# Two of four float32 value units of an attention projection on TensorE's float16 path

## The chip, the core and the metric

The kernel runs on one core of one Trainium2 chip. The metric is the device time of one execution in microseconds (us); lower is better.

## The reference, cut to what matters

One step of a two-layer decoder trunk, for a prompt of 256 tokens and 8 samples of one new token each (past length 256), with shared weights, all in float32. Layer 0 uses sparse softmax attention (8 heads of 128; a ReLU indexer picks 64 keys for each query and the rows are gathered, for the samples from a paged cache), layer 1 an RG-LRU. A ConvGLU follows each, with RMSNorms before and one at the end. The part around the change is this:

```python
q, k, v, qi, ki, wi = jnp.split(a @ w_in, ATTN_SPLITS, axis=-1)   # a: (256 + 8 tokens, 1024)
q, k = rope(q, pos), rope(k, pos)                                 # also qi, ki
idx, valid = indexer_topk(qi, wi, ki, q_pos, n_keys, 64)
logits = einsum(q, gather(k, idx)) * HEAD_DIM ** -0.5             # invalid: -inf
o = einsum(softmax(logits), gather(v, idx))
```

## The kernel before

The 264 tokens lie in the free dimension, the features in the partitions. Every projection is cut into **units** of 128 output columns: one unit is one PSUM bank of `acc` (128x264), summed over 8 chunks of 128 input features. The 27 units of the attention's input projection are ordered by hand in `ORDER`: 0 to 8 are the indexer and q0 to q5, 9 and 10 are v0 and v1, 11 and 12 are q6 and q7, 13 to 16 are v2 to v5, 17 to 24 are k0 to k7, and 25 and 26 are v6 and v7. Units 27 to 34 are the output projection.

**A normal unit** multiplies in float16 halves. SyncE loads the float32 weights (512 KB) into one of four slots of `stage`. ScalarE makes the high half, float16(512 w), in `hi` (L593). VectorE makes the low half, float16(512 w - high), in `lo` (L997). TensorE then runs three float16 matmuls for each chunk, 24 in all: high by `aH`, high by `aL`, low by `aH` (`unit`, L1535, L1538, L1541).

**A raw unit** (`RAW_V`, units 13 to 16) skips both halves: its weights go straight to `raw_v`, and TensorE multiplies them in float32 with `x32`, a float32 copy of the normalized input that ScalarE makes a chunk at a time (L786). That is 8 matmuls of two records each in the trace (`unit_raw`, L1506). All four are loaded together once a scratch area is free, and share the semaphore `raw_in` (L462).

**Each engine walks a loop over steps u**, one for each unit, and does in that step what the hand-made order gives it; each engine executes strictly in order. What matters around the change:
- TensorE: unit u, then the small matmuls and transposes of the step. `heads_of_step(u)` turns one value or key head token-major (L1616, L1617): v0 at step 11, v1 at 12, v2 at 14, v3 at 15, v4 at 16, k0 to k7 at steps 19 to 26. Before the n-th such turn it waits until ScalarE has copied out the one before (`kv_kept`). For a value it waits too until ScalarE has evicted its unit (`v_read`). `turn_picked` (L1706) spreads the samples' picked row numbers inside unit 14. `spread_queries` runs inside unit 15, `turn_weights` inside unit 22, `sample_values` inside units 23 and 24.
- ScalarE: `swap_halves(u)` (L703, L704) for the rotary embedding of a q or k unit, `keep_turned` (L691) for the turn of the step before, `keep_v(u)` (L714, L715) for a value unit, then `hi(u+4)`. Step 12 starts with three parameter copies (L772, L774), step 13 with `qrep` (L778), which waits until q7 is rotated.
- VectorE: `rope(u)` (L1080, L1081) multiplies with cosine and sine; `take_merged` (L1105 to L1109) does eight rounds of max, index and replace that find the samples' 64 keys, the eighth in step 11 after `rope(12)`; `take_second` does the same for the prompt; `sample_dots(j)` (L1136), steps 15, 16, 16 and 17, multiplies gathered keys with the samples' queries; then `lo(u+4)`.
- GpSimd: the subtraction that ends a rotation (L2046, signals `roped`), in step 12 also `row_numbers` (L2026 to L2030, signals `phys_done`), which needs the last round of `take_merged`; in step 16 the eight gathers of cache rows (L2020), the four of values after unit 16 is done.

The four matmul banks are reused in turn, so unit u also waits until bank u - 4 has been read.

Of the kernel before, what the change touches and what calls it, by code (L numbers as in the profile page):

```python
# [16 lines left out]
ALU = mybir.AluOpType  # L17
ACT = mybir.ActivationFunctionType
# [7 lines left out]
D = 1024  # L26
# [38 lines left out]

RAW_V = U_V[2:6]
SPLIT_AT = {u: u - SLOTS for u in range(SLOTS, U_OUT + SLOTS) if u not in RAW_V}

# [114 lines left out]
def build(nc, a, o):  # L183
    with ExitStack() as ctx:
# [92 lines left out]
        kxT = area1[:, 4608:4608 + D].rearrange("p (r n) -> p r n", r=8)  # L277

        spareH = zH[:, DC:FC, :].rearrange("p c t -> p (c t)").bitcast(F32)
        spareL = zL[:, DC:FC, :].rearrange("p c t -> p (c t)").bitcast(F32)  # L280
# [112 lines left out]
        idx_mm, idx_relu, bias_done = sem("idx_mm"), sem("idx_relu"), sem("bias_done")  # L393
        gidx_done, kx_turned, kx_kept = sem("gidx_done"), sem("kx_turned"), sem("kx_kept")
        kx_in = sem("kx_in")
        kg_in = [sem(f"kg_in{i}") for i in range(4)]
        vg_in = [sem(f"vg_in{i}") for i in range(4)]
        qz_zero = sem("qz_zero")
        ss_mm, ss_relu, sc_mm = sem("ss_mm"), sem("ss_relu"), sem("sc_mm")
# [180 lines left out]
        def _(act):  # L580
# [136 lines left out]
            def after_heads(u):  # L717
# [8 lines left out]
                if LG + 5 <= u and u != INSIDE + 1:  # L726
                    o_high(u - LG - 5)

            for u in range(LAST_STEP + 1):
                if u == 3:  # L730
                    act.wait_ge(unit_done, U_W + 1)
                    nc.scalar.copy(wiT[:], acc[ID:ID + IH, U_W % 4, 0:T]).then_inc(wi_kept, 1)
# [12 lines left out]
                if u == 6:  # L745
                    act.wait_ge(qz_zero, 1)
                    act.wait_ge(roped, 3)
                    for half in range(2):
                        rows_ = slice(ID * half, ID * half + ID)
                        places = qz[rows_, :].rearrange("p (s m) -> p m s", s=NS)  # L750
                        for b in range(2):
                            ins = nc.scalar.copy(places[:, b:b + 3:2, :], qiT[ID * b:ID * b + ID, :, TP:T])
                    ins.then_inc(ki_twice, 1)
                    act.wait_ge(idx_mm, 2)
                    nc.scalar.activation(relu0[:, 1::2, :], E[:, TP:2 * TP].rearrange("p (h k) -> p h k", h=2), ACT.Relu).then_inc(idx_relu, 1)
# [45 lines left out]
                if u < U_OUT and u not in U_V:  # L801
                    swap_halves(u)
                if u == 21:
                    act.wait_ge(smx_done, 1)
                    nc.scalar.activation(sl[:], sl[:], ACT.Exp).then_inc(sexp_done, 1)
# [182 lines left out]
        def _(dve):  # L988
# [157 lines left out]
            for u in range(LAST_STEP + 1):  # L1146
# [4 lines left out]
                if u == 3:  # L1151
                    dve.wait_ge(roped, 3)
                    v.tensor_copy(kiT[ID:P, :], kiT[0:ID, :]).then_inc(ki_twice, 1)
                if u == 22:
                    dve.wait_ge(sp_turned, 1)
# [84 lines left out]
                if u == 11:  # L1240
                    take_merged(6, 1)
                    rope(12)
                    take_merged(7, 1, found=True)
                if 16 <= u < 18:
                    sample_dots(u - 14)
                if u == 20:

# [240 lines left out]
        def _(pe):  # L1488
# [10 lines left out]
            def unit_raw(u, between):  # L1499
# [9 lines left out]
                ins.then_inc(unit_done, 1)  # L1509

            def unit(u, xH, xL, bank=None, first=True, last=True, x0=0, ready=None, rest_ready=None, between=None):

                n, cols = shape(u)
                if u in RAW_V:
                    unit_raw(u, between)
                    return
# [234 lines left out]
            for u in range(2, U_OUT + 1):  # L1751
                if u == 3:
                    pe.wait_ge(x_kept, 2)
                if u < U_OUT:
                    if u in (23, 24):
                        between = lambda i: sample_values(4 * (u - 23) + i // 4, i % 4)
                    elif u == 5:
                        between = lambda i: index_products() if i == 6 else None
                    elif u == 6:
                        between = lambda i: late_scores() if i == 4 else None  # L1760
                    elif u == 14:
                        between = lambda i: turn_picked() if i == 8 else None
                    elif u == 15:
                        between = lambda i: spread_queries() if i == 4 else None
                    elif u == 22:
                        between = lambda i: turn_weights() if i == 8 else None
# [41 lines left out]
                if u != INSIDE:  # L1808
                    heads_of_step(u)
                if u == 20:  # L1810
                    pe.wait_ge(qb_read, 4)
# [107 lines left out]
        def _(pool):  # L1919
# [34 lines left out]
            g.memset(ones[:], 1.0).then_inc(ones_set, 1)  # L1954
            g.memset(qz[:], 0.0).then_inc(qz_zero, 1)
            pool.wait_ge(pages_in, 32)
            g.tensor_scalar(gidx[:], ptc[:], 8.0, blkc[:, 0:1], ALU.mult, ALU.add).then_inc(gidx_done, 1)
            pool.wait_ge(gidx_done, 1)
            g.indirect_dma_start(out=kx, out_offset=None, in_=a["cache_kidx"].rearrange("a n (b r) d -> (a n b) (r d)", b=8),
# [72 lines left out]
            def biases():  # L2032
# [7 lines left out]
                g.tensor_scalar(seld[:], ident[0:NS, 0:NS], selnew[:, 0:1], None, ALU.mult).then_inc(phys_done, 1)  # L2040

            for u in range(LG + 1 + H):
                if u < U_OUT and u not in U_V:
                    dst, part = roped_home(*KIND[u])
# [127 lines left out]
```

## Time and profile before

| | |
|---|---|
| median of 3 runs | 591.82 us (591.76 to 592.20) |
| the profiled execution | 592.18 us |
| its span, first to last instruction | 590.4 us |
| instructions | 12747 |
| TensorE busy / VectorE / ScalarE / GpSimd | 579.4 / 453.6 / 369.7 / 226.8 us |
| mean granted TensorE clock | 0.996 of full speed |
| HBM read, written | 108.8 MB, 3.9 MB |

A matmul's busy time overlaps the next one's, since matmuls are pipelined; the pitch from one start to the next tells what it costs. Times in a timeline count from the start of the span. The stretch of the change is 44 to 110 us, units 9 to 25.

### The profile page before, as it was taken

How to read it: one execution, taken by the hardware profiler on the slowest of the kernel's cores; microseconds unless marked ns; L12 is line 12 of the kernel's file. 1: busy time of each engine (PE TensorE's matmuls, PEld its weight loads, DVE VectorE, ACT ScalarE, POOL GpSimd, SP SyncE). 2: the span in 40 equal slices, each digit the busy share in tenths (PEclk: the TensorE clock that was granted, in tenths of full speed). 3: DMA queues.
4: the chain of work that ended last, by engine and by line, in shares of the span. 5: the costliest groups of instructions: out<-in, count | busy, mean ns of one | idle time of the engine just before them, and what ended most of it. 6: DMA issues, size and time to landing. Idle time of an engine off the chain costs nothing.

```text
span 590.4 us, 12747 instructions
## 1 busy us (share of the span) xinstructions
PE 579.4 (98%) x5015; PEld 502.8 (85%) x5015; DVE 453.6 (77%) x904; ACT 369.7 (63%) x629; POOL 226.8 (38%) x230
## 2 busy tenths in 40 slices
PE   7999999999999999999999999999999999999995
PEld 7888889888888888888888888888888888888885
DVE  4899996666897778787778898789878777885542
ACT  6985566676765666575555788856756566654322
POOL 4241466713354544551000112273644555432220
PEclk9999999999999999999999999999999999999998
DMA  9959694329766766678997952065766666879602
GB/s 264 263 137 278 184 339 133 108 80 324 209 200 194 198 195 195 197 226 244 259 264 216 239 170 73 1 179 172 207 193 199 192 195 199 233 220 240 175 7 74
DMA packets 205420, 113.28 MB, mean 192 GB/s; under 512 B 5561, under 2 KB 202217, under 8 KB 205337
## 3 DMA queue, kind: packets, MB, share of 16 engines
q1 hardware_dynamic: 203169, 106.33, 63.9%
q0 software_dynamic: 1680, 5.79, 2.8%
q8 instruction: 40, 0.66, 0.5%
q10 hardware_dynamic: 512, 0.35, 0.2%
q14 instruction: 19, 0.16, 0.1%
HBM read 108.83 MB, written 3.86 MB: 191 GB/s over the span
## 4 chain that ended last, share of the span: by engine, by line
PE 92%; DVE 3%; POOL 1%; ACT 1%; issue 1%; DVEq 0%; ACTq 0%; POOLq 0%
PE acc L1538 25%; PE acc L1535 25%; PE acc L1541 25%; PE acc L1506 2%; PE acc L1726 1%; PE acc L1728 1%; PE acc L1727 1%; PE misc L1897 1%; PE acc L1561 1%; DVE w_lo L997 1%; PE misc L1663 1%; POOL hT L1930 1%; ACT w_hi L593 1%; PE misc L1642 1%; PE misc L1626 1%
## 5 line engine op out<-in xcount | busy, mean ns | idle before, releaser
L1535 PE MATMUL acc<-aH,w_hi 128*128 128x264 f16 (+1 forms) x886 | 244.5, 276 | 0.8 <-DVE work L1310 0.7
L1538 PE MATMUL acc<-aL,w_hi 128*128 128x264 f16 (+1 forms) x886 | 244.5, 276 | 0.0
L1541 PE MATMUL acc<-aH,w_lo 128*128 128x264 f16 (+1 forms) x886 | 244.5, 276 | 0.0
L997 DVE SCALAR_TENSOR_TENSOR w_lo<-stage,w_hi 128x1024 f16<-128x1024 f32 (+1 forms) x155 | 205.7, 1332 | 30.4 <-ACT w_hi L593 29.9
L593 ACT ACTIVATE w_hi<-stage 128x1024 f16<-128x1024 f32 (+1 forms) x155 | 171.1, 1109 | 32.4 <-PE acc L1541 25.2
L1535 PE MATMUL acc<-zH,w_hi 128*128 128x264 f16 x384 | 106.0, 276 | 0.0
L1538 PE MATMUL acc<-zL,w_hi 128*128 128x264 f16 x384 | 106.0, 276 | 0.0
L1541 PE MATMUL acc<-zH,w_lo 128*128 128x264 f16 x384 | 106.0, 276 | 0.0
L1538 PEld LDWEIGHTS acc<-aL,w_hi 128*128 128x128 f16 (+1 forms) x886 | 88.1, 99 | 13.5
L1535 PEld LDWEIGHTS acc<-aH,w_hi 128*128 128x128 f16 (+1 forms) x886 | 86.8, 98 | 14.5 <-issue 1.5
L1541 PEld LDWEIGHTS acc<-aH,w_lo 128*128 128x128 f16 (+1 forms) x886 | 88.1, 99 | 12.6
L2016 POOL TENSOR_TENSOR scratch<-work,r0z 128x264 f32<-128x264 f32 x44 | 65.5, 1488 | 75.2 <-ACT work L891 75.2
L2014 POOL COPY ftail<-scratch 128x10 f32<-128x10 f32 x44 | 49.1, 1116 | 35.3 <-DVE scratch L1328 35.0
L885 ACT ACTIVATE work<-scratch,fprm 128x264 f32<-128x264 f32 x44 | 26.7, 608 | 48.8 <-DVE scratch L1328 48.6
L1328 DVE TENSOR_TENSOR scratch<-acc,rinv 128x264 f32<-128x264 f32 x44 | 19.0, 432 | 39.3 <-PE acc L1541 39.2
L1535 PEld LDWEIGHTS acc<-zH,w_hi 128*128 128x128 f16 x384 | 37.6, 98 | 5.6
L1541 PEld LDWEIGHTS acc<-zH,w_lo 128*128 128x128 f16 x384 | 37.6, 98 | 5.6
L1538 PEld LDWEIGHTS acc<-zL,w_hi 128*128 128x128 f16 x384 | 37.6, 98 | 5.6
L891 ACT ACTIVATE work<-work 128x264 f32<-128x264 f32 x44 | 18.6, 423 | 35.0 <-DVE work L1341 35.0
L1946 POOL TENSOR_TENSOR sqsum<-sqsum,sq 128x264 f32<-128x264 f32 x18 | 16.0, 886 | 54.6 <-ACT sq L615 54.0
L607 ACT ACTIVATE aH<-hT,gcol 128x264 f16<-128x264 f32 x24 | 12.3, 514 | 32.7 <-DVE hT L1361 18.2
L2046 POOL TENSOR_TENSOR area<-area,scratch 128x264 f32<-128x264 f32 x16 | 17.6, 1102 | 31.4 <-DVE area L1081 31.4
(421 smaller groups left out, 951.7 us busy)
## 6 DMA issues: line engine op xcount, KB each, us to landing
stage<-in_w_ffn_up SPq DMA_DIRECT2D x88, 512.0 KB, 4.7
stage<-in_w_ffn_down SPq DMA_DIRECT2D x32, 704.0 KB, 5.7
stage<-in_w_attn_in SPq DMA_DIRECT2D x22, 512.0 KB, 6.6
stage<-in_w_rec_in SPq DMA_DIRECT2D x16, 512.0 KB, 4.9
stage<-in_w_attn_out SPq DMA_DIRECT2D x8, 512.0 KB, 3.8
stage<-in_w_rec_out SPq DMA_DIRECT2D x8, 512.0 KB, 3.8
area<-in_w_attn_in SPq DMA_DIRECT2D x4, 512.0 KB, 4.6
area<-in_x_prompt SPq DMA_DIRECT2D x2, 512.0 KB, 4.6
```

The lines of the kernel that those rows point to most:

```text
L593: nc.scalar.activation(halves_of(u)[0], stage[:, s, 0:n, 0:cols], ACT.Copy, scale=WSCALE).then_inc(hi_done, 1)
L885: nc.scalar.activation(c32[:, p, :], gs[:, p, :], ACT.Identity, scale=fprm[layer][:, FROW_W + 2, j:j + 1], bias=fprm[layer][:, FROW_B, j:j ...
L891: nc.scalar.activation(c32[:, p, :], c32[:, p, :], ACT.Gelu_apprx_tanh).then_inc(gelu_done, 1)
L997: v.scalar_tensor_tensor(low, stage[:, place_in_line(u) % 4, 0:n, 0:cols], WSCALE, high, ALU.mult, ALU.subtract).then_inc(lo_done, 1)
L1328: v.tensor_tensor(gs[:, p, :], acc[:, u % 4, 0:T], rinv[:], ALU.mult).then_inc(acc_read, 1)
L1535: t_.matmul(out, high[:, c, :], xH[:, x0 + c, :], start=first and c == 0, stop=False)
L1538: t_.matmul(out, high[:, c, :], xL[:, x0 + c, :], start=False, stop=False)
L1541: ins = t_.matmul(out, low[:, c, :], xH[:, x0 + c, :], start=False, stop=last and c == n - 1)
L1946: g.tensor_tensor(sqsum[:], sqsum[:], sq[:, c % 2, :], ALU.add).then_inc(ss_done, 1)
L2014: g.tensor_copy(ftail[:, :, j], gs[:, p, TP - 2:T]).then_inc(tail_copied, 1)
L2016: g.tensor_tensor(gr[:, p, :], c32[:, p, :], r0z[:], ALU.mult).then_inc(gr_done, 1)
L2046: g.tensor_tensor(dst, dst, rot[0:part, (before(u) + 1) % 2, :], ALU.subtract).then_inc(roped, 1)
```

## The change

Units 13 and 14 (v2, v3) stop being raw. Their weights are still loaded raw, with the two that stay raw, in `raw_v`. ScalarE makes both high halves in step 11. GpSimd makes the low half of v2 in two passes (multiply by 512 in place, then subtract) and half of the low half of v3. VectorE makes the other half of v3's in one instruction, after `rope(12)`. The halves lie in a part of `zH` and `zL` that is idle then. TensorE multiplies them in float16, all 16 high products first and the 8 low ones after. `turn_picked`, two of the four `sample_dots`, the samples' softmax, `turn_weights` and `sample_values` move up to a unit later. Two semaphores are renamed or replaced to make room.

```diff
+HALVED_V = RAW_V[:2]
...
+        half_v = [[z[:, 0:DC, :].rearrange("p c t -> p (c t)")[:, j * D:(j + 1) * D].rearrange("p (c n) -> p c n", c=DC)
+                   for z in (zH, zL)] for j in range(len(HALVED_V))]
...
+            def high_of_value(j):
+
+                act.wait_ge(raw_in, 16 * len(RAW_V))
+                nc.scalar.activation(half_v[j][0], raw_v[:, j], ACT.Copy, scale=WSCALE).then_inc(v_hi, 1)
+
             for u in range(LAST_STEP + 1):
+                if u == 11:
+                    high_of_value(0)
...
                 if u == 6:
-                    act.wait_ge(qz_zero, 1)
+                    act.wait_ge(mask_set, 1)
...
                 if u < U_OUT and u not in U_V:
                     swap_halves(u)
-                if u == 21:
+                if u == 11:
+                    high_of_value(1)
+                if u == 22:
                     act.wait_ge(smx_done, 1)
                     nc.scalar.activation(sl[:], sl[:], ACT.Exp).then_inc(sexp_done, 1)
...
-                if u == 22:
+                if u == 23:
                     dve.wait_ge(sp_turned, 1)
...
                 if u == 11:
                     take_merged(6, 1)
                     rope(12)
+                    dve.wait_ge(v_hi, 2)
+                    dve.wait_ge(v_lo, 1)
+                    v.scalar_tensor_tensor(half_v[1][1][:, DC // 2:, :], raw_v[:, 1, DC // 2:, :], WSCALE, half_v[1][0][:, DC // 2:, :],
+                                           ALU.mult, ALU.subtract).then_inc(v_lo, 1)
                     take_merged(7, 1, found=True)
-                if 16 <= u < 18:
-                    sample_dots(u - 14)
-                if u == 20:
+                if u in (17, 19):
+                    sample_dots(2 + (u - 17) // 2)
+                if u == 21:
...
+            def unit_value(u, j):
+
+                high, low = half_v[j]
+                out = acc[:, u % 4, 0:T]
+                pe.wait_ge(v_hi, j + 1)
+                bank_free(u)
+                for c in range(DC):
+                    t_.matmul(out, high[:, c, :], aH[:, c, :], start=c == 0, stop=False)
+                    t_.matmul(out, high[:, c, :], aL[:, c, :], start=False, stop=False)
+                pe.wait_ge(v_lo, 1 + 2 * j)
+                for c in range(DC):
+                    ins = t_.matmul(out, low[:, c, :], aH[:, c, :], start=False, stop=c == DC - 1)
+                ins.then_inc(unit_done, 1)
...
-                    if u in (23, 24):
-                        between = lambda i: sample_values(4 * (u - 23) + i // 4, i % 4)
+                    if u in (24, 25):
+                        between = lambda i: sample_values(4 * (u - 24) + i // 4, i % 4)
...
-                    elif u == 14:
-                        between = lambda i: turn_picked() if i == 8 else None
                     elif u == 15:
-                        between = lambda i: spread_queries() if i == 4 else None
-                    elif u == 22:
+                        between = lambda i: turn_picked() if i == 2 else spread_queries() if i == 4 else None
+                    elif u == 23:
                         between = lambda i: turn_weights() if i == 8 else None
...
-                if u == 20:
+                if u == 21:
                     pe.wait_ge(qb_read, 4)
...
-            g.memset(qz[:], 0.0).then_inc(qz_zero, 1)
+            small(g.memset(qz[:], 0.0))
...
+            def low_of_value(j, chunks):
+
+                pool.wait_ge(v_hi, j + 1)
+                small(g.tensor_scalar(raw_v[:, j, chunks, :], raw_v[:, j, chunks, :], WSCALE, None, ALU.mult))
+                g.tensor_tensor(half_v[j][1][:, chunks, :], raw_v[:, j, chunks, :], half_v[j][0][:, chunks, :],
+                                ALU.subtract).then_inc(v_lo, 1)
+
             for u in range(LG + 1 + H):
+                if u == 11:
+                    low_of_value(0, slice(0, DC))
+                if u == 12:
+                    low_of_value(1, slice(0, DC // 2))
                 if u < U_OUT and u not in U_V:
                     dst, part = roped_home(*KIND[u])
                     pool.wait_ge(acc_read, before(u) + 1)
```

## Rows read from the trace of the kernel before

**Rows 1.** The page: busy time, share of the span and instructions.
```profile
PE 579.4 (98%) x5015; PEld 502.8 (85%) x5015; DVE 453.6 (77%) x904; ACT 369.7 (63%) x629; POOL 226.8 (38%) x230
```

**Rows 2.** Waits of PE from 50 to 130 us (total us, times, longest).
```profile
PE misc L1616 <- DVE zL L1128: 0.4, 1, 0.4
```

**Rows 3.** PE's timeline, units 12 to 15 (start us, duration).
```profile
54.26 0.27 PE L1535 MATMUL acc<-aH,w_hi 128*128 128x264 f16 x1
...
56.96 0.27 PE L1616 MATMUL misc<-ca,scratch 128*128 128x128 f32 x1
...
57.17 3.06 PE L1506 MATMUL acc<-scratch,area 128*128 128x264 f32 x13
...
60.74 2.39 PE L1506 MATMUL acc<-scratch,area 128*128 128x264 f32 x10
...
64.91 0.27 PE L1616 MATMUL misc<-ca,scratch 128*128 128x128 f32 x1
```

**Rows 4.** Line L462 (raw loads), window 47.7 to 48.9 us.
```profile
L462 SPq DMA_DIRECT2D area<-in_w_attn_in x2: 380/771/1162, 47.4 to 47.8; - x2
...
DMA to landing us min/median/max: 4.4/4.9/5.5
```

**Rows 5.** ACT's timeline, steps 11 to 13.
```profile
50.85 0.52 ACT L786 ACTIVATE r0z<-hT,gcol_w 128x264 f32<-128x264 f32 x1
53.20 0.38 ACT L703 COPY scratch<-acc 64x264 f32<-64x264 f32 x1 [1.84 <-PE acc L1541]
...
53.98 0.95 ACT L772 COPY fprm<-misc 128x440 f32<-128x440 f32 x2
...
55.14 0.40 ACT L691 COPY area<-misc 128x256 f32<-128x256 f32 x1
...
60.03 1.14 ACT L778 COPY area<-area 128x512 f32<-128x512 f32 x2 [2.12 <-POOL area L2046]
...
61.41 0.39 ACT L715 ACTIVATE scratch<-acc 128x264 f32<-128x264 f32 x1
61.68 1.06 ACT L593 ACTIVATE w_hi<-stage 128x1024 f16<-128x1024 f32 x1
```

**Rows 6.** POOL's timeline, steps 8 to 18.
```profile
46.30 0.74 POOL L2046 TENSOR_TENSOR area<-area,scratch 128x264 f32<-128x264 f32 x1 [1.15 <-DVE area L1081]
57.19 0.74 POOL L2046 TENSOR_TENSOR area<-area,scratch 128x264 f32<-128x264 f32 x1 [10.15 <-DVE area L1081]
59.26 0.74 POOL L2046 TENSOR_TENSOR area<-area,scratch 128x264 f32<-128x264 f32 x1 [1.33 <-DVE area L1081]
...
62.08 0.44 POOL L2030 TENSOR_SCALAR zL<-idxf 8x64 f32<-8x64 f32 x1
...
83.26 1.66 POOL L2046 TENSOR_TENSOR area<-area,scratch 128x264 f32<-128x264 f32 x1 [2.67 <-DVE area L1081]
```

**Rows 7.** Groups of POOL instructions, shapes apart (busy us, mean ns).
```profile
L1999 POOL TENSOR_TENSOR fpre<-fprm 128x176 f32<-128x176 f32 x2 | 1.1, 560 | 0.0
...
L1981 POOL TENSOR_SCALAR eps<-eps 128x264 f32<-128x264 f32 x1 | 0.9, 881 | 0.1
...
L1972 POOL TENSOR_SCALAR pt8f<-pt 8x2 f32<-8x2 int32 x1 | 0.2, 228 | 0.0
```

**Rows 8.** Line L2071 of POOL, window 122.0 to 122.5 us (ns min/median/max).
```profile
L2071 POOL TENSOR_SCALAR work<-work,prcp,r0tok x2: 447/500/553, 122.1 to 122.5; 128x128 f32<-128x128 f32 x1, 128x256 f32<-128x256 f32 x1
```

**Rows 9.** DVE's timeline, steps 8 and 11.
```profile
46.34 1.78 DVE L997 SCALAR_TENSOR_TENSOR w_lo<-stage,w_hi 128x1024 f16<-128x1024 f32 x1
...
56.34 0.43 DVE L1080 TENSOR_TENSOR scratch<-scratch,ca 128x264 f32<-128x264 f32 x1
...
58.41 0.43 DVE L1080 TENSOR_TENSOR scratch<-scratch,ca 128x264 f32<-128x264 f32 x1
```

**Rows 10.** PE's timeline, the turn of k1 in step 20.
```profile
85.66 0.27 PE L1616 MATMUL misc<-ca,area 128*128 128x128 f32 x1
```

More of the change, by code:

```diff
@@ L393, in build @@
         idx_mm, idx_relu, bias_done = sem("idx_mm"), sem("idx_relu"), sem("bias_done")
-        gidx_done, kx_turned, kx_kept = sem("gidx_done"), sem("kx_turned"), sem("kx_kept")
+        v_hi, kx_turned, kx_kept = sem("v_hi"), sem("kx_turned"), sem("kx_kept")
         kx_in = sem("kx_in")
@@ L397, in build @@
         vg_in = [sem(f"vg_in{i}") for i in range(4)]
-        qz_zero = sem("qz_zero")
+        v_lo = sem("v_lo")
         ss_mm, ss_relu, sc_mm = sem("ss_mm"), sem("ss_relu"), sem("sc_mm")
@@ L1509, in unit_raw @@
                 ins.then_inc(unit_done, 1)
+            def unit_value(u, j):
[10 more added lines that the diff above has]
+                ins.then_inc(unit_done, 1)
             def unit(u, xH, xL, bank=None, first=True, last=True, x0=0, ready=None, rest_ready=None, between=None):
                 n, cols = shape(u)
+                if u in HALVED_V:
+                    unit_value(u, HALVED_V.index(u))
+                    return
                 if u in RAW_V:
@@ L1954, in _ @@
             g.memset(ones[:], 1.0).then_inc(ones_set, 1)
-            g.memset(qz[:], 0.0).then_inc(qz_zero, 1)
+            small(g.memset(qz[:], 0.0))
             pool.wait_ge(pages_in, 32)
-            g.tensor_scalar(gidx[:], ptc[:], 8.0, blkc[:, 0:1], ALU.mult, ALU.add).then_inc(gidx_done, 1)
-            pool.wait_ge(gidx_done, 1)
+            small(g.tensor_scalar(gidx[:], ptc[:], 8.0, blkc[:, 0:1], ALU.mult, ALU.add))
             g.indirect_dma_start(out=kx, out_offset=None, in_=a["cache_kidx"].rearrange("a n (b r) d -> (a n b) (r d)", b=8),
```

## The prediction

> **What bounds the kernel now.** Look first at the busy shares on the page: TensorE is busy for 579.4 us of the 590.4 us span [rows 1]. Then ask for TensorE's waits in the stretch of the change: from 50 to 130 us it waits once, for 0.4 us [rows 2]. So every microsecond taken from TensorE's own work is a gain there, and every new wait of TensorE is a loss of its full length. The work around it can only do harm. The third view is therefore each engine's timeline from unit 11 to unit 15, where I follow the change.
>
> **What TensorE saves.** Unit 12 shows the float16 price: 54.26 to 56.96, 2.70 us for 24 matmuls [rows 3]. Raw unit 13 runs from 57.17 to the start of unit 14 at 60.74, 3.57 us. Two units change form: 2 x (3.57 - 2.70) = **1.74 us saved**. Unit 14 with `turn_picked` takes until 64.91, so that spread costs 4.17 - 3.57 = 0.60 us; it moves to unit 15 at the same price. The turns and later sample products keep their prices too, a unit later.
>
> **ScalarE, first new wait.** Both high halves wait for all four raw loads. The last is issued at 47.8 and lands 5.5 us later, at 53.3 [rows 4]. ScalarE is ready at 50.85, where its last x32 chunk stood; that chunk now queues behind the first high half [rows 5]. In order: high half of v2, 1.06 us (the row of L593), to 54.36; the x32 chunk 0.52, to 54.88; the swap of q6, 0.78 (53.20 to 53.98), to 55.66; high half of v3, 1.06, to 56.72; the parameter copies 1.16 (53.98 to 55.14), to 57.88; and the copy of turned v0, 0.40, to 58.28 instead of 55.54. TensorE wants to turn v1 at 56.96 and needs that copy gone: it waits **1.32 us**, where it had 1.4 us to spare. (Neighbouring copies overlap by up to 0.1 us, so 1.1 is as likely.) Unit 13 then starts at 57.17 + 1.32 = 58.49.
>
> **GpSimd, what a pass costs.** No row shows 128x1024 elements on this engine. For the two-input pass: 176 columns take 0.56 us [rows 7] and 264 take 0.74 [rows 6], 2.05 ns a column and 0.20 fixed, so 1024 columns take 2.3 us and 512 take 1.25. Its second input is float16, which no row has; I take it as float32. For the one-input multiply by a constant, the same form is L1981: 264 columns in 0.88 us, against 0.23 for two columns, so 2.5 ns a column [rows 7]; 1024 columns are 2.78 us, 512 are 1.5. The other end is L2071, whose factors are per-partition operands: 0.45 us for 128 columns, 0.55 for 256 [rows 8], 0.83 ns a column, so 1.2 us and 0.77. I take L1981, since its operands have the form of the new instruction, and keep L2071 for the other end.
>
> The Trainium skill ("GPSIMD Engine Reference", § 4.1 Engine selection) calls one-input work roughly line-rate, which speaks for the cheap end; L1981 disagrees and L2071 agrees. By the page the sum would be the 0.9 us of the second case below.
>
> **GpSimd against VectorE.** At 46.34 VectorE's low half takes 1.78 us: a GpSimd subtraction had begun at 46.30 and ran to 47.04, and VectorE finished 1.08 us after that [rows 6, 9]. So one of these blocks the other for its whole length. The new passes and `rope(11)`, `rope(12)` and VectorE's half of v3 will take turns. By this I place the work:
> - GpSimd multiplies v2 from 54.37 to 57.15. `rope(11)`, due at 56.34 [rows 9], goes first after that, to 57.58. GpSimd subtracts from 57.58 to 59.9: `v_lo` is 1.
> - VectorE needs 2.07 us from one rope to the next (56.34 to 58.41), so it is ready for `rope(12)` at 59.2, waits to 59.9, ends its first product at 60.35. GpSimd's subtraction of q6 runs to 61.1. VectorE's half of v3 (half of 1.08, some 0.6) runs to 61.7.
> - GpSimd multiplies half of v3, 61.7 to 63.2, and subtracts, 63.3 to 64.55: `v_lo` is 3. The subtraction of q7 ends at 65.3. Before, it ended at 60.0 [rows 6]; it is 5.3 us late.
>
> Without turn-taking it would end at about 63.9, so blocking is 1.4 us of this. The Trainium skill ("SBUF — State Buffer", § Who interferes with whom) states the same exclusive lock for a VectorE instruction with two SBUF inputs against a GpSimd one that reads SBUF; the 1.78 us row agrees.
>
> **What TensorE then waits for.** Unit 13 needs `v_lo` 1 after its 16 high products, at 58.49 + 1.80 = 60.3: it has been there since 59.9, no wait. Unit 14 starts at 61.19 and needs `v_lo` 3 at 62.99: it comes at 64.55, **1.56 us**. It ends at 65.45. Next is the turn of v2, which needs ScalarE's `keep_v` of unit 13. ScalarE stands at `qrep`, which waits for q7's subtraction, with the copy of v1 and `keep_v` queued behind it. Before, from 60.00 to the end of L715 at 61.80 that is 1.80 us [rows 5, 6]. Now 65.3 + 1.8 = 67.1, so **1.65 us** more. Unit 15 starts at 67.32 (a turn is 0.21: 56.96 to 57.17). Before it would have started, without the 0.60 of `turn_picked`, at 65.12 - 0.60 = 64.52.
>
> **Sum.** 1.32 + 1.56 + 1.65 - 1.74 = **2.8 us lost** at unit 15.
>
> **Behind unit 15.** `row_numbers` ends 2.5 us after q7's subtraction (60.00 to 62.52), so at 67.8; `turn_picked` comes at 67.32 + 2 x 0.45 = 68.2. No wait, where the old place would have waited. Picks and cache gathers are then some 5.2 us later than before (`turn_picked` stood at 60.74 + 5 x 0.45 = 63.0), TensorE only 2.8. The tightest follower is the turn of k1 at 85.66, whose subtraction on GpSimd ended at 84.92 [rows 6, 10]: 0.74 us of slack. The moved `sample_dots` leave before `rope(17)` and `rope(18)` one set of dots less each, some 1.9 us (8 x 0.21 and the bias), so I cost this part at nothing. What hides it is that slack and that move, and if both are gone the last rival's price is due. VectorE's added 0.6 us goes the same way. The samples' softmax, exponent and weights shift together with their readers by one unit: nothing. The changed start-up semaphores: GpSimd idles for 10.15 us before 57.19 and far more at the start, nothing.
>
> **The numbers.** The profiled execution has a span of 590.4 us and a time of 592.18, 1.78 outside the span, and is 0.36 above the median of the runs. The span becomes 593.2, that execution 595.0, the median 591.82 + 2.8 = **594.6 us**. A measurement of this kernel can tell about 0.2% from no change, 1.2 us.
>
> **The cases.**
> 1. *As summed*, 594.6 (593.6 to 595.6): chance 0.53. For it: ScalarE is shown waiting 2.12 us for that subtraction already [rows 5], so any lateness goes through in full.
> 2. *GpSimd multiplies cheaply*, at 1.2 and 0.77 us. The same placing gives: v2's low half at 58.0, `rope(11)` held until then, v3's half at 62.1, VectorE's at 62.7, q7's subtraction at 63.45, the turn of v2 at 65.25, unit 15 at 65.47. That is 0.9 us lost, 592.7: chance 0.22, nearly all of it within 0.2%. It also holds the mix of costlier passes and an earlier landing. If only the ScalarE wait remained, the change would end at 1.32 - 1.74, 0.4 us gained.
> 3. *The conversions hide*, the faster side: copy of v0 by 56.96 and `keep_v` of unit 13 by 57.17 + 5.40 = 62.57. Then no TensorE wait is left and all of the 1.74 us shows: 590.1. It decides at a landing of 52.0 instead of 53.3 and q7's subtraction by 60.8 instead of 65.3. GpSimd's 10.15 us of idle time speaks for it; the placing, in which even the cheap multiply misses by 2.7 us, against it. Chance 0.13.
> 4. *The picks come too late*: the gathers' further 5.2 - 2.8 = 2.4 us go through VectorE's dots to the rotation of k1, less 0.74 of slack: 1.7 us more, 596.3. Chance 0.12.
>
> The range reaches from 591.4 (case 3 out) to 596.0 (most of case 4 in). Faster 0.13; same 0.20, case 2 less its upper edge; slower 0.67.
>
> **What would show it.** In the changed profile: L1506 with 32 records instead of 64, and 48 float16 ones at 0.1125 us pitch. TensorE's list of waits, one row now, should have three new ones: on ScalarE's L691 (about 1.3), on GpSimd's low half in unit 14 (1.6), on ScalarE's L715 (1.7). GpSimd's 128x1024 multiply should take 2.8 us and its subtraction 2.3; `qrep` should start near 65.3. If the multiply is 1.2 us, case 2 holds. If TensorE shows no waits at L1616, the prediction is wrong in sign. If waits sit beyond 80 us, case 4 holds.

## The result and the profile after

| | before | after |
|---|---|---|
| median | 591.98 us (4 runs, 591.76 to 592.20) | 598.99 us (4 runs, 596.66 to 600.32) |
| ratio | | 1.0112 (95%: 1.0100 to 1.0123) |
| profiled execution | 592.18, span 590.4 | 596.66, span 594.9 |

The change costs 7.0 us. The direction was forecast, the size was not: 2.8 us were forecast, and 599.0 lies above the range. The profiled execution of after is the shortest of its four, 2.3 us under the median, so the profile shows only 4.5 of the 7.0 us. The rest is looked for in another profile below.

The page, busy time per engine, to set beside [rows 1]:

```profile
PE 577.8 (97%) x5031; PEld 500.0 (84%) x5031; DVE 457.0 (77%) x905; ACT 371.8 (63%) x631; POOL 234.1 (39%) x234
```

TensorE does 1.6 us less work, as meant. What it waits for in after from 50 to 130 us (total us, times, longest), one row of 0.4 us before [rows 2]:

```profile
PE misc L1649 <- ACT area L694: 3.4, 3, 1.7
PE misc L1649 <- ACT scratch L718: 1.4, 1, 1.4
PE acc L1538 <- POOL zL L2076: 0.4, 1, 0.4
PE misc L1658 <- DVE nmx L1131: 0.3, 1, 0.3
```

PE's timeline says where (start, duration; the bracket is the wait ahead of it). L1649 is the turn, L1616 before [rows 3, 10]:

```profile
58.07 0.30 PE L1649 MATMUL misc<-ca,scratch 128*128 128x128 f32 x1 [1.28 <-ACT area L694]
...
63.38 1.07 PE L1538 MATMUL acc<-aH,zL 128*128 128x264 f16 x8 [0.40 <-POOL zL L2076]
...
65.88 0.33 PE L1649 MATMUL misc<-ca,scratch 128*128 128x128 f32 x1 [1.42 <-ACT scratch L718]
...
89.19 0.30 PE L1649 MATMUL misc<-ca,area 128*128 128x128 f32 x1 [1.72 <-ACT area L694]
...
101.47 0.30 PE L1649 MATMUL misc<-ca,area 128*128 128x128 f32 x1 [0.42 <-ACT area L694]
```

The first three waits are the three forecast ones: the turn of v1, `v_lo` 3 in unit 14, the turn of v2. The last two, at the turns of k1 and k4, lie where the forecast had put nothing. (The 0.3 us on `nmx` comes later still, at 125.7 us.) The same turns give the bill. At the turn of k0 after is 1.64 us behind before (84.39 against 82.75), at k1 3.53 (89.19 against 85.66), at k6 4.48 (114.01 against 109.53), and 4.5 is the difference of the spans.

GpSimd's timeline, the passes that no row of before had shown (compare [rows 6, 7]):

```profile
54.30 2.79 POOL L2075 TENSOR_SCALAR area<-area 128x1024 f32<-128x1024 f32 x1 [7.58 <-ACT zH L735]
57.17 2.13 POOL L2076 TENSOR_TENSOR zL<-area,zH 128x1024 f16<-128x1024 f32 x1
59.25 0.94 POOL L2087 TENSOR_TENSOR area<-area,scratch 128x264 f32<-128x264 f32 x1
60.16 1.93 POOL L2075 TENSOR_SCALAR area<-area 128x512 f32<-128x512 f32 x1
62.17 1.16 POOL L2076 TENSOR_TENSOR zL<-area,zH 128x512 f16<-128x512 f32 x1
63.28 0.74 POOL L2087 TENSOR_TENSOR area<-area,scratch 128x264 f32<-128x264 f32 x1
```

And the late part, in the chain that ended last and on ScalarE's timeline: a load of the stage buffer takes 10.8 us to land, ScalarE's high half waits for it with the copy that TensorE's turn of k1 needs (L694) queued behind. The five input-projection loads that before has from 68 to 92 us take 7.2 us at the median; after's six take 9.3. In before ScalarE waits for no load of the stage from 56 to 100 us.

```profile
76.92 10.78 DMA stage<-in_w_attn_in
```
```profile
87.72 1.06 ACT L596 ACTIVATE w_hi<-stage 128x1024 f16<-128x1024 f32 x1 [2.38 <-DMA stage<-in_w_attn_in]
88.69 0.35 ACT L694 COPY area<-misc 128x256 f32<-128x256 f32 x1
```

Three questions follow. Are the waits in front of unit 15 the change's price, as forecast? What costs 3 us behind it? And why do the runs spread over 3.7 us, when those of before spread over 0.4?

### The profile page after: what moved, and what is told of

Its sections match the earlier page's. It is cut to its first block, busy times and chain, and to the rows that moved or that the text cites. A ratio compares the mean times of both kernels' runs of the same rounds, so it can differ in the third digit from the quotient of the medians.

```text
span 594.9 us, 12788 instructions
## 1 busy us (share of the span) xinstructions
PE 577.8 (97%) x5031; PEld 500.0 (84%) x5031; DVE 457.0 (77%) x905; ACT 371.8 (63%) x631; POOL 234.1 (39%) x234
## 4 chain that ended last, share of the span: by engine, by line
PE 76%; DVE 7%; ACT 6%; DMA 4%; POOL 2%; issue 2%; SPq 1%; ACTq 0%; DVEq 0%
PE acc L1574 23%; PE acc L1571 23%; PE acc L1568 23%; DVE w_lo L1009 3%; ACT w_hi L596 3%; DMA stage<-in_w_attn_in 2%; PE misc L1928 1%; PE acc L1759 1%; PE acc L1761 1%; PE acc L1760 1%; DMA area<-in_w_attn_in 1%; DMA area<-in_x_prompt 1%; POOL area L2075 1%; PE misc L1696 1%; POOL hT L1961 1%
```

## The experiments

Each ratio is against runs of the kernel before on the same chip, whose medians were 591.97 to 592.12. Where the runs of a kernel spread, the ratio differs from the quotient of the two medians. All medians and intervals:

| run | what | us | ratio (95%) |
|---|---|---|---|
| e1_moves | before, the moves alone | 595.68 | 1.0075 (1.0050 to 1.0099) |
| e2_free | after, no conversions | 593.55 | 1.0031 (1.0020 to 1.0042) |
| e3_actfirst | after, ScalarE's copy of qrep last | 596.75 | 1.0082 (1.0065 to 1.0099) |
| e4_again | after | 598.93 | 1.0108 (1.0085 to 1.0130) |
| e5_picked | before, turn of the picks moved | 593.79 | 1.0040 (1.0025 to 1.0055) |
| e6_dots | before, dots and softmax moved | 594.11 | 1.0039 (1.0024 to 1.0053) |
| e7_back | after, dots and softmax back | 596.67 | 1.0082 (1.0065 to 1.0099) |
| e8_freeback | e2, dots and softmax back | 592.30 | 1.0011 (0.9998 to 1.0023) |
| e9_freestill | e2, no move at all | 592.04 | 1.0007 (0.9998 to 1.0017) |
| e10_fill | after, TensorE busy in one wait | 597.45 | 1.0098 (1.0081 to 1.0115) |
| e11_half16 | before, half of unit 16 in halves | 592.58 | 1.0007 (0.9998 to 1.0016) |
| e12_one16 | before, unit 16 in halves | 594.10 | 1.0040 (1.0026 to 1.0053) |
| e13_light | before, VectorE less 5 search rounds | 592.21 | 1.0004 (0.9995 to 1.0014) |
| e14_lightfree | e9, the same rounds out | 592.02 | 1.0008 (0.9997 to 1.0018) |
| e15_lightmoves | e1, the same rounds out | 595.58 | 1.0062 (1.0045 to 1.0079) |
| e16_lightafter | after, the same rounds out | 598.83 | 1.0112 (1.0095 to 1.0129) |
| e17_qkb | e11, scaling of the dots on ScalarE | 592.40 | 1.0008 (0.9999 to 1.0017) |
| e18_halfdots | e8, half of the dots | 592.22 | 1.0007 (0.9996 to 1.0018) |

### Moves against conversions

**e1_moves.** The kernel before with the diff's hunks for `turn_picked`, `sample_dots`, the softmax and what reads it, and no others.

> All four value units stay raw; only the moves of turn_picked, two sample_dots, the samples' softmax and its readers are made. Theory A (the loss behind unit 15 is a late release of the stage loads, which the conversions cause): nothing moves, 591.9 us within 0.2%, no wait of TensorE at the turn of k1. Theory B (the moves themselves cost the 2.9 us that are lost behind unit 15): about 594.8 us, with that wait.

595.68. The moves alone cost 3.7 us at the median, which the forecast had put at nothing. Up to the turn of k0 the profile is level with before; behind it come five small waits of 0.3 to 0.4 us. The profiled execution (594.51) is the shortest of four that reach to 597.99, so its trace shows 2.3 us of the loss. The clock does not explain that spread: the execution of 596.58 has a mean clock of 0.998.

**e2_free.** The other half: the changed kernel with nothing converted; the values of heads 2 and 3 are left out.

```
-    high_of_value, low_of_value and VectorE's half of v3
+    for z in (zH, zL): g.memset(z[:, 0:DC, :], 0.0)      at the start
```

> Units 13 and 14 in float16, but nobody makes their halves (they are zeros, set by GpSimd in its idle time at the start, so v2 and v3 and what follows from them are left out). Theory A: the 1.74 us of TensorE come out in full, 590.2 us, and no new wait. Theory B: TensorE's saving is partly lost whatever the conversions do, because the moves cost it: 591.9 us or more.

593.55. At the turn of k0 this run is 2.0 us ahead of before (80.76), TensorE's saving in full; then it waits 1.8 us at k1 and 0.4 at k4, and ends slower than before. So the conversions cost about 5.4 us of after's median (598.99 less 593.55; what the clock adds behind their waits is in it), and even for nothing they bring no gain in this order.

**e3_actfirst.** ScalarE's copy of `qrep`, which waits for q7's subtraction, is moved to the end of step 13.

```
-                if u == 13: (at the head of the step)
-                    act.wait_ge(roped, before(U_K[0]))
-                    for t in range(2): ... nc.scalar.copy(qrep[:, t], ...)
+                (the same lines, behind hi() of the step)
```

> The changed kernel, but in step 13 ScalarE does the copy of turned v1, keep_v and the high half of unit 17 before qrep, so these don't wait for GpSimd's subtraction of q7. Theory A: the 1.4 us wait at the turn of v2 goes, the low half of unit 17 is 3 to 4 us earlier, the load it releases too, and the waits at the turn of k1 (1.7 us) and in the units around it go: span 591.7 or less against 594.9, clock 0.996. Theory C (the gathers, which stay late, are what delays the later units): only the 1.4 us come back, 597.5 us.

596.75, with runs from 596.5 to 597.6. The 1.4 us wait at the turn of v2 is gone, but `turn_picked` then waits 1.8 us for the row numbers (L1739 on POOL zL), since these stand behind GpSimd's conversions too. One wait took the other's place. The profiled execution (596.92, clock 0.998) is no shorter than the profiled one of after (596.66, 0.996). The median is 2.2 us lower, and the clock (next section) is the likely reason: three of the four executions here have 0.997 or 0.998, and six of after's eight do not reach 0.996.

### The spread: TensorE's clock

**e4_again.** The changed kernel, unchanged.

> The changed kernel as it is, to see another execution's trace. If its granted clock is below 0.996 again, the trace should show a stretch at a lower clock behind one of the new waits, of 4 to 8 us; that would be the difference between 596.7 and 600.3 us.

598.93, and its profiled execution (599.06) is one of the long ones. The granted clock in stretches of 4 us; the columns are the stretch's length, busy us and count of PE, PEld, DVE, ACT and POOL, then clock, DMA share, GB/s. First e4_again:

```profile
64.00:68.00 4.00, 2.57 (x11) 1.41 (x9) 1.09 (x2) 3.85 (x9) 2.05 (x6) 0.79 0.00 0
68.00:72.00 4.00, 4.00 (x15) 3.31 (x15) 3.11 (x11) 0.98 (x3) 1.72 (x2) 0.50 0.64 145
72.00:76.00 4.00, 4.00 (x18) 3.34 (x17) 3.90 (x20) 1.86 (x5) 2.23 (x3) 0.86 0.81 256
```

and the profiled run of after:

```profile
64.00:68.00 4.00, 2.58 (x15) 1.71 (x13) 1.12 (x1) 3.94 (x9) 1.97 (x6) 1.00 0.00 0
68.00:72.00 4.00, 4.00 (x25) 3.48 (x24) 3.79 (x12) 2.01 (x7) 2.27 (x3) 1.00 0.66 170
```

Both have the same idle TensorE of 1.4 us from 64.5 to 66. In one the granted clock then falls, to 0.50, the 1.2 GHz level, from 68 to 72 us, and v3 is turned at 74.56 instead of 71.20: 3.4 us lost. The program is the same. The end is only 2.4 us later (span 597.3 against 594.9), because the 1.7 us wait at k1 is not there: TensorE comes later to that turn (90.66). e16_lightafter below has the same waits in front of unit 15 and the same three clocks, 0.79, 0.50 and 0.86. Of the eight timed executions of after the two shortest (596.66, 596.82) have a mean clock of 0.996, the other six (598.6 to 600.3) 0.989 to 0.995; that these six all lost it behind this wait is inferred, since only one of them was profiled. Before has no such wait, a mean clock of 0.996 to 0.998, and a spread of 0.4 us in the four runs beside after (at most 1.2 in any later set).

**e10_fill.** TensorE is given work in that wait.

```
+                if u == 14:
+                    bank_free(15)
+                    for _ in range(12):
+                        t_.matmul(acc[:, 15 % 4, 0:T], half_v[0][0][:, 0, :], aH[:, 0, :], start=True, stop=True)
```

> The changed kernel with 12 matmuls of float16 more (128x128 by 264 columns, into the bank of unit 15, which the first matmul of that unit overwrites) right after unit 14, where TensorE waits 1.4 us for the turn of v2. Theory C (the executions at 599 to 600 are those in which the granted clock fell to half behind this wait): TensorE works through the wait, the clock does not fall, and the median is 596.5 to 597 with a spread under 1 us, 2 us less for 12 instructions more. Rival: the spread comes from the loads behind unit 16, and the median stays at 598.5 to 599.5.

597.45, from 596.21 to 598.97, clocks of 0.995 to 0.998. The wait at the turn of v2 is gone and the median 1.5 us lower, but the intervals of this run and of after overlap, and a spread of 2.8 us is left. The clock explains part at most: the longest execution, 598.97, has 0.996. The waits at v1 and k1 are still there. What the rest of this spread is stays open.

### Which move costs

**e5_picked** has the hunk of `turn_picked` alone on the kernel before, **e6_dots** the other hunks of e1_moves.

> The kernel before with one of the moves alone: the turn of the picks (turn_picked) from the middle of unit 14 to early in unit 15; dots, softmax and values of the samples stay where they were, nothing is halved. Theory P (the late picks carry the cost of the moves: picks, row numbers, gathers and dots all start 2.3 us later, and VectorE's and ScalarE's halving of weights behind them is late for TensorE's turns at units 17 to 20): 594.5 to 596.5, with TensorE waits at the turns of k2 and k4 as in the run with all moves. Theory D (the dots and the softmax that stand a step later carry it): 591.8 to 592.5, no new wait over 0.3 us.

> The kernel before with the other moves alone: dots 2 and 3 in steps 17 and 19, softmax, its turn and the samples' values a step later; the turn of the picks stays in unit 14, nothing is halved. Theory P: 591.8 to 592.5. Theory D: 594 to 596, with the turn of the weights (md, seld) waiting for the softmax and ScalarE's exponential late for the turn of k4.

593.79 and 594.11: 1.8 and 2.1 us, and 3.7 together in e1_moves. Neither theory of a single culprit holds; the two add. The new waits of e5_picked are on GpSimd, at the turn of k1 (L1616) and at the turn of the samples' weights (L1712):

```profile
PE misc L1616 <- POOL area L2044: 0.9, 1, 0.9
PE misc L1712 <- POOL seld L2038: 0.6, 1, 0.6
```

and those of e6_dots on the softmax (0.3 at L1712), on what comes late behind it (0.4 at the turn of k4) and on VectorE (0.7 at L1625). In e5_picked ScalarE also waits for loads of the stage, 1.8 us in two waits, where before has none.

**e7_back.** The changed kernel with the hunks of e6_dots undone.

> The changed kernel with the dots, softmax and samples' values back in the steps of before; the turn of the picks stays in unit 15 and the conversions stay. Theory P with slow stage loads: no gain, 598 to 600, waits at the turns of k1 and k4 as in the changed kernel. Theory D: 2 to 3 us less than the changed kernel, 596 to 597. A third possibility: slower than the changed kernel by 1 us or more, because dots 2 and 3 would stand in VectorE's queue before their gathers have landed.

596.67, 2.3 us less than after at the median. That looks like the price of the moved dots and softmax alone, but the traces do not bear it out. The profiled execution (596.77, clock 0.997) is level with that of after (596.66, 0.996): its wait at k1 is longer (2.3 us for 1.7, behind a load of 11.4 us) and the one at k4 is gone. The medians differ because executions with a clock of 0.992 or 0.993 end at 596.6 and 597.3 here and at 598.6 or later in after. Why they do was not looked into, so what the moved dots cost in the changed kernel is not shown.

**e8_freeback.** The same hunks undone in e2_free.

> The run with free halves (units 13 and 14 read halves that are set to zero once, no conversion; values of two heads are left out), with dots, softmax and samples' values back in the steps of before. Theory P or slow loads: as that run, 593 to 594. Theory D: TensorE's saving of 1.74 us comes through, 590 to 591. If it is 592, half of the loss behind unit 15 is the moves and half the loads that crowd with the gathers.

592.30, 1.25 us less than e2_free and level with before; the spans of the two profiles, 590.4 and 591.5, say the same. So far the costs could simply add: TensorE saves 1.74 us, the moved turn of the picks costs 1.8. The next run tests this.

### Can TensorE's saving come through at all?

**e9_freestill.** Now `turn_picked` too is back, in the middle of unit 14's high products.

```
-                    elif u == 15: turn_picked at i == 2
+                    elif u == 14: turn_picked between chunks 3 and 4 of unit_value
```

> Units 13 and 14 read halves that are set to zero once (no conversion; values of two heads are left out), and nothing is moved at all: the turn of the picks is back in the middle of unit 14, as before. If the costs simply add (TensorE saves 1.74 us, the turn of the picks costs 1.8, the dots and softmax 2.1), this is 590.2 to 590.6, and it is the most that the change could ever have gained. If the saving is lost at the stage loads whatever the order is (loads that crowd with the gathers), it is 591.7 to 592.3.

592.04. The best case of the idea, conversions for nothing and no move, gains nothing, so the costs do not simply add. TensorE now waits 1.7 us for the row numbers:

```profile
PE misc L1733 <- POOL zL L2058: 1.7, 1, 1.7
```

They are ready at 61.95 us here, at 62.13 in e14_lightfree and at 62.52 in before, where TensorE wanted them at 63.05. The picks' search runs on VectorE and the row numbers on GpSimd, a chain of its own that had just met TensorE's in the kernel before.

The wait has the same effect on the clock as in after, in some executions: seven of the eleven end at 591.7 to 592.4 with clocks of 0.997 or 0.998, four at 593.3 to 593.9 with 0.994 or 0.995. The profiled execution is one of the four (593.3): 0.81 from 60 to 64 us and 0.76 from 64 to 68. e14_lightfree's has the same wait and 1.00 throughout, and turns v2 at 64.47 instead of 65.94: the clock cost 1.5 us here.

**e11_half16** and **e12_one16** look for a version that gains: nothing moved, and only the last raw unit split, where conversions fit into idle time (12 splits all eight chunks).

```
+HALVED_V = RAW_V[3:]
+    step 11, ScalarE: high half of chunks 0 to 3 (12: of 4 to 7 behind swap_halves)
+    step 11, GpSimd: multiply and subtract chunks 0 to 3, ahead of q6 (12: multiply 4 to 7
+        behind row_numbers, subtract them behind the gathers of the keys)
```

> The kernel before, nothing moved; of unit 16 alone (the last raw unit) the first four chunks are split into halves: ScalarE's high (512 columns) at the start of step 11, GpSimd's multiply and subtraction (1.5 and 1.2 us) before the sixth query head's rope. By the rows nobody waits for either engine there. TensorE saves half of 0.87 us, so 591.5 to 591.7 if nothing is late; 592.0 if the 0.4 us are lost behind; above 592.5 if GpSimd's subtraction holds VectorE's rope back.

> The same with all eight chunks of unit 16: second high where ScalarE is idle (2.1 us behind step 11), second multiply behind the row numbers, second subtraction behind the gathers of the keys. TensorE saves 0.87 us and its turns stand where they stood, so 591.1 to 591.4 if nothing is late; 592.0 or more if the second subtraction holds back VectorE's first dots or the gathers of the values.

592.58 and 594.10. No gain in the first, which has one new wait, 0.7 us for `seld`; the second waits 0.8 us for the low half (the gathers of the keys end too late for it), 0.8 at the turn of k1 and 0.6 for `seld`, both GpSimd's.

**e13 to e16**: the theory was that VectorE, busy 3.8 to 4.0 of every 4 us from 64 to 88 us, is a second bound. One edit in four kernels; the search of the second query tile is left out but for one round.

```
-                if 13 <= u < 16:
-                    take_second(2, last=u == 15)
+                if u == 15:
+                    take_second(1, last=True)
```

> The kernel before without five of the six search rounds that VectorE makes for the second query tile in steps 13 to 15 (MAX8 and MATCH_REPLACE8 on 128x256, some 4.7 us of VectorE; the picks of the second tile are left out but for one round). Theory V (two bounds side by side): TensorE stood without a wait there, so 591.6 to 592.1, as before. If it falls under 591, VectorE alone was the bound.

> Free halves without moves (units 13 and 14 read zeros) and the same five search rounds left out. Theory V: TensorE's saving comes through at last, 590.1 to 590.7 against 592.0 with the rounds. Rival (loads that crowd with the gathers, or GpSimd's chain of gathers and rope, take it whatever VectorE does): 591.7 to 592.3.

> The moves alone (turn of the picks, dots, softmax), nothing halved, with the same five search rounds left out. Theory V: the 3.7 us of the moves fall to 0 to 1 us, so 592 to 593. Rival (the cost is GpSimd's and the loads'): 595 to 596.

> The changed kernel with the same five search rounds left out. Theory V: what is left is the waits in front of unit 15 (1.3, 0.4 and 1.4 less 1.74 saved) and the clock behind them: 593 to 596 against 599. Rival: 597.5 to 599.

592.21, 592.02, 595.58, 598.83: nothing moves in any of the four. The theory falls in this form. In e14 the 1.7 us wait for the row numbers is the same as in e9; in e15 most of the 3.6 us is a 2.0 us wait at k1, behind a load of the stage that ScalarE waits 2.7 us for. The traces say why the cut did nothing: it frees VectorE before 72 us, where it then waits for the first gathered keys (4.6 us in e15). The first gather starts when the cast of the row numbers is done. Here is that cast (gix) and the end of the first and the last of the four dots (qkb) on VectorE's timeline, first in before:

```profile
64.63 0.17 DVE L1188 CAST gix<-gbias 128x4 uint32<-128x4 f32 x1
71.54 0.23 DVE L1139 TENSOR_SCALAR qkb<-qk,gbias 128x8 f32<-128x8 f32 x1
...
82.27 0.23 DVE L1139 TENSOR_SCALAR qkb<-qk,gbias 128x8 f32<-128x8 f32 x1
```

then in e8_freeback, where TensorE is 1.7 us ahead:

```profile
64.93 0.17 DVE L1196 CAST gix<-gbias 128x4 uint32<-128x4 f32 x1
71.76 0.23 DVE L1147 TENSOR_SCALAR qkb<-qk,gbias 128x8 f32<-128x8 f32 x1
...
82.28 0.23 DVE L1147 TENSOR_SCALAR qkb<-qk,gbias 128x8 f32<-128x8 f32 x1
```

and in e5_picked, where only the turn of the picks is later:

```profile
66.59 0.17 DVE L1188 CAST gix<-gbias 128x4 uint32<-128x4 f32 x1
73.43 0.23 DVE L1139 TENSOR_SCALAR qkb<-qk,gbias 128x8 f32<-128x8 f32 x1
...
83.94 0.23 DVE L1139 TENSOR_SCALAR qkb<-qk,gbias 128x8 f32<-128x8 f32 x1
```

The dots follow the picks, not TensorE: 2.0 us later picks are 1.7 to 1.9 us later dots.

**e17_qkb** is e11_half16 with VectorE relieved behind the landing of the gathered keys; nothing is left out.

```
-                small(ins)
-                v.tensor_scalar(qkb[:, j, :], qk[:, j, :], SCALE, gbias[:, 4 + j:5 + j], ...).then_inc(qb_read, 1)
+                ins.then_inc(qb_read, 1)
+    ScalarE, end of step 19: four activations (Identity, scale, bias) of qk into qkb
```

> As the run that halves the first four chunks of unit 16 (592.6), with the four scalings of the samples' dots (qkb, 0.26 us each on VectorE, and the waits of VectorE for its own last dot) done by ScalarE at the end of step 19 instead. Theory V: VectorE is 1 us lighter, the turn of the weights is no longer late, 591.4 to 591.8. If ScalarE's later halves are held back by the wait for the last dot, 592.5 to 593.5.

592.40 (591.5 to 593.5). In its profile TensorE has no new wait and the span is 589.7, 0.7 under that of before, but this is the shortest of 11 runs and their median is level. A gain of 0.4 us, TensorE's saving in this version, can't be told from none.

**e18_halfdots** takes much more from VectorE at the place that counts; four heads of eight are left out of each dot.

```
-                for h in range(H):
+                for h in range(0, H, 2):
```

> As the run with free halves and the dots and softmax in the steps of before (592.3), with four of the eight heads in each of the four dots left out (16 of 32 dots of 0.21 us, 3.4 us of VectorE between 70 and 82 us). Theory V2 (from the landing of the first gathered keys VectorE is the second bound): the waits of 0.9 us at the turn of k1 and 0.9 us at the turn of the weights, both for GpSimd's work on what VectorE hands on, vanish, and TensorE's 1.74 us come through: 590.3 to 590.8. Rival (the gathers and the loads that crowd with them): the waits stay and it is 592.0 to 592.5.

592.22, the rival's number. But not with the rival's rows. The two waits on GpSimd of e8_freeback,

```profile
PE misc L1737 <- POOL seld L2064: 0.9, 1, 0.9
PE misc L1641 <- POOL area L2077: 0.9, 1, 0.9
```

are gone as theory V2 wanted, and one has come in their place:

```profile
PE misc L1642 <- ACT area L694: 1.3, 1, 1.3
```

It is ScalarE's copy behind a high half that waits 1.9 us for a load of the stage (in e8_freeback it waited 1.8 us in two waits). The whole of 72 to 88 us, in before, then in e18_halfdots (columns as above):

```profile
72.00:88.00 16.00, 16.00 (x136) 13.91 (x135) 15.78 (x65) 10.23 (x22) 9.62 (x8) 1.00 1.03 345
```
```profile
72.00:88.00 16.00, 14.73 (x130) 12.64 (x129) 12.70 (x41) 9.72 (x19) 11.02 (x10) 1.00 1.08 351
```

VectorE falls from 15.8 to 12.7 us of 16; the DMA engines stay full, 345 and 351 GB/s. The kernel before is on several edges here at once: TensorE 16.0, VectorE 15.8, and the DMA engines full. The waits on GpSimd in e5_picked and e8_freeback hang on VectorE: they are gone when VectorE has less to do.

## Why the prediction was right and wrong

**"What TensorE saves"**, 1.74 us: right. At the turn of k0 e2_free is 1.99 us ahead, 0.27 of which it had at the turn of v1 already (56.69 against 56.96): 1.72.

**"ScalarE, first new wait"**, 1.32 us: measured 1.28, by the order that the text laid out.

**"GpSimd, what a pass costs"**: 2.79 us for the multiply (forecast 2.78), 2.13 and 1.16 for the subtractions (2.3 and 1.25). The 512-column multiply was 1.93 for 1.5, but in e11_half16, where no two-input instruction of VectorE runs beside it, it takes 1.51: the price was right, and the 0.4 us more come from the work beside it. So the cost came from the row with the same operand form, and the cheap end, case 2, did not happen. The Trainium skill ("GPSIMD Engine Reference", § 4.1 Engine selection) calls one-input work roughly line-rate. At 2.7 ns a column (2.79 us for 1024) this pass is slower than the two-input one at 2.1, so the measurement speaks against it.

**"GpSimd against VectorE"**: too strict. VectorE's rope(11) and rope(12), two inputs in SBUF each, and its half of v3:

```profile
56.00 0.43 DVE L1092 TENSOR_TENSOR scratch<-scratch,ca 128x264 f32<-128x264 f32 x1
58.81 0.77 DVE L1092 TENSOR_TENSOR scratch<-scratch,ca 128x264 f32<-128x264 f32 x1 [0.78 <-ACT scratch L707]
59.85 0.89 DVE L1257 SCALAR_TENSOR_TENSOR zL<-area,zH 128x512 f16<-128x512 f32 x1
```

The first ran its usual 0.43 us in the middle of GpSimd's multiply; the second, under the subtraction, took 0.77. The third was still running when GpSimd began the multiply of v3 at 60.16, and that is the multiply that took 1.93 instead of 1.51. In e12_one16 VectorE's low half began 0.27 us into a multiply of 1.49 and took 1.42, against 1.23 elsewhere in that trace. So the two engines lengthen each other's instructions here by 0.2 to 0.4 us, each by less than the overlap, and do not take turns for whole instructions. The Trainium skill ("SBUF — State Buffer", § Who interferes with whom) lets a VectorE instruction with two SBUF inputs contend with any GpSimd one that reads SBUF; the one-input multiply read SBUF and did not block VectorE at 56.00.

So q7's subtraction ended at 64.0, not 65.3 (the prediction's own 63.9 "without turn-taking" was the better number), and `v_lo` 3 cost **0.40 us instead of 1.56**. This is the term of the sum that was mis-sized. The turn of v2 cost 1.42 for 1.65.

**"Sum"**, 2.8 us lost at unit 15. The waits are 1.28 + 0.40 + 1.42 = 3.10, less 1.74 is 1.4. By the turns of v3 (71.20 against 69.56, and 0.34 ahead at unit 12) it is 2.0; each restart behind a wait costs 0.2 us more than the wait shown (unit 12 ends at 56.62 in after and v1 is turned at 58.07, 1.45 later, with a wait of 1.28), which is most of the difference. As a kind this part held, and it ended 0.8 us too high.

**"Behind unit 15 ... I cost this part at nothing"** is the step that failed. The profiled run loses 2.9 us there and the moves alone cost 3.7 at the median. The step looked for the slack of one follower, 0.74 us on GpSimd at k1, and judged the moved dots to be relief for VectorE. It read no view of VectorE and the DMA engines from 72 to 88 us, where both are full: the picks' chain starts the gathers and the dots, and the gathers share the DMA engines with the loads of the stage (in before, from 68 to 92 us, the gathers' queue takes 43% of their time and the loads' 55%). With it falls the premise of the first paragraph, that every microsecond taken from TensorE's work is a gain there: e9_freestill takes 1.74 us away, moves nothing, and gains nothing.

Case 4 had the right start (late picks), with 1.7 us; e5_picked measures 1.8, and its wait at k1 is on GpSimd's rotation, as case 4 has it. That the numbers lie so close is in part luck, since case 4 has one wait behind picks that are 2.4 us late, and e5_picked has two (0.9 and 0.6) behind picks that are 2.0 late. In after itself the wait at k1 is on ScalarE's copy behind a load of the stage, a path that no case had. Case 4's chance of 0.12 was too low, and it had no companion for the moved softmax and dots, 2.1 us alone. Why one load takes 10.8 us was not tested.

**What no case had** is the clock. Three waits were priced at their length. In e4_again the 1.4 us wait was followed by half clock and cost 3.4 us more, of which 2.4 are left at the end. By the mean clocks this happened in six of eight executions, and it is the likely reason for most of the difference between the profiled run (4.5 us lost) and the median (7.0).

So the 7.0 us are, by the profiled run, 1.6 in front of unit 15 (2.0 less the 0.3 by which after was ahead at unit 12), 2.9 behind it, and 2.5 that most runs have beyond it. In e4_again, which lies nearer to the median, the 6.9 us of its span are 5.0 by the turn of v3 and 1.9 behind it. Added up from these, either miss alone leaves the range, which ends at 596.0: with the clock lost and nothing behind unit 15 it is 592.0 + 1.6 + 3.4 = 597.0, with the clock kept it is 592.0 + 1.6 + 2.9 = 596.5.

What stays open: whether the loads alone would take TensorE's saving if both VectorE and GpSimd had room (e18_halfdots points to it, in one trace), and where the spread in e1_moves and what is left of it in e10_fill come from. No version tried beats the kernel before; after in particular is not mended by the order of ScalarE (e3_actfirst) or by undoing the dots (e7_back).

## What to carry to other kernels

An engine without waits is not the only bound. Before pricing what it would save, ask for the busy shares of the other engines and of the DMA engines in the stretch *behind* the edit, and for the time at which each chain that starts there is pinned; here even a free conversion gained nothing. A wait on a fully busy TensorE is to be priced with the clock that may fall behind it. And a step that is "only moved" is late work for its followers: the moves, of one unit each, cost more (3.7 us) than the float16 units saved (1.74). Last, before two medians with different mean clocks are subtracted, compare executions with the same clock: e3_actfirst and e7_back seem to gain 2.2 us over after, and in executions with a clock of 0.996 or more they gain next to nothing (596.5 to 596.9 and 596.3 to 596.8, against 596.7 and 596.8).

## What the runs showed of the hardware

- A one-input multiply of GpSimd by a constant (float32, in place) takes 2.79 us for 128x1024 (after) and 1.51 for 128x512 (e11_half16), longer than its two-input subtraction into float16 (2.13 and 1.16).
- The multiply left VectorE's two-input product at 0.43 us; the subtraction stretched it to 0.77. A multiply of 512 columns that began while VectorE's two-input low half ran took 1.93 us (after), 1.51 without it.
- TensorE idle for 1.4 us can be followed by a granted clock of 0.50 over 68 to 72 us (e4_again, e16_lightafter) or by none (after, e7_back): same idle time. The same holds behind 1.7 us: 0.81 and 0.76 in e9_freestill, 1.00 in e14_lightfree.
- From 72 to 88 us the DMA engines are full in before and in after (1.03 of their time in both, 345 and 356 GB/s), and yet a 512 KB load of the stage took at most 8.5 us in before, 10.8 in after and 11.4 in e7_back. The share of busy time does not tell them apart.
